# Seven block products in place of eight for 20 of the 22 gate and up column pairs of a SwiGLU, in a float32 decoder layer on one core

## The reference, cut to what matters

```python
def swiglu(x, w_gate, w_up, w_down):
    return (jax.nn.silu(x @ w_gate) * (x @ w_up)) @ w_down

for l in range(DEPTH):                                    # DEPTH is 1
    mix = hybrid_mixer(x, ...)                            # pooling, RG-LRU, short conv, gates
    x = layer_norm(ALPHA * x + mix, ln_g[l, 0], ln_b[l, 0])
    xa = memory_cross_attention(x, mem, ...)
    x = layer_norm(ALPHA * x + xa, ln_g[l, 1], ln_b[l, 1])
    ff = swiglu(x, ffn_w_gate[l], ffn_w_up[l], ffn_w_down[l])
    x = layer_norm(ALPHA * x + ff, ln_g[l, 2], ln_b[l, 2])
```

## Time and profile before

| | us |
|---|---|
| median of 3 runs | 1055.01 (1054.86 to 1055.73) |
| the profiled execution | 1056.62 |
| its span | 1054.7 |
| PE busy | 1040.6 (99%) |
| PEld busy | 878.9 (83%) |
| DVE busy | 509.9 (48%) |
| ACT busy | 388.3 (37%) |
| POOL busy | 44.7 (4%) |
| HBM read | 108.09 MB, 104 GB/s over the span |

### The profile page before, as it was taken

One profiled execution on the slowest core, in us unless ns is written; L12 is line 12 of the kernel. 1 busy time (PEld: TensorE's weight loads), 2 busy tenths in 40 slices (PEclk: granted clock), 3 DMA queues, 4 the chain that ended last, 5 costly groups with the idle time before them and its releaser, 6 DMA issues.

```text
span 1054.7 us, 12863 instructions
## 1 busy us (share of the span) xinstructions
PE 1040.6 (99%) x5020; PEld 878.9 (83%) x5020; DVE 509.9 (48%) x709; ACT 388.3 (37%) x527; POOL 44.7 (4%) x37
## 2 busy tenths in 40 slices
PE   8999999999999999999999999999999999999997
PEld 7888888888888888888889998898888888888886
DVE  4668585876432423344865564752222322243336
ACT  4455646355422222233543352542222222232222
POOL 2000000000000000000400000130000000000000
PEclk9999999999999999999999999999999999999999
DMA  5324233142432332325143331243323232222311
GB/s 203 106 82 133 80 99 119 60 122 77 160 120 80 98 101 80 120 80 212 68 160 121 120 120 41 80 159 98 102 82 117 80 115 84 98 101 81 118 41 80
DMA packets 88706, 110.65 MB, mean 105 GB/s; under 512 B 2125, under 2 KB 81121, under 8 KB 88673
## 3 DMA queue, kind: packets, MB, share of 16 engines
q1 hardware_dynamic: 86704, 103.82, 30.3%
q0 software_dynamic: 1824, 6.32, 1.7%
q10 hardware_dynamic: 144, 0.05, 0.0%
HBM read 108.09 MB, written 2.10 MB: 104 GB/s over the span
## 4 chain that ended last, share of the span: by engine, by line
PE 95%; DVE 2%; ACT 1%; POOL 1%; issue 1%; DVEq 0%; POOLq 0%
PE ps L462 32%; PE ps L464 31%; PE ps L463 31%; PE ps L491 1%; POOL wl L425 1%; DVE xnat L1142 1%; DVE xT_l L1100 0%; ACT ps L851 0%; PE ps L696 0%; DVE probs L1133 0%; ACT wh L825 0%; POOL rows L418 0%; DVE wl L1092 0%; DVE xnat L1123 0%; ACT xT_h L831 0%
## 5 line engine op out<-in xcount | busy, mean ns | idle before, releaser
L1092 DVE TENSOR_TENSOR wl<-raw,wh 128x1024 fp32r<-128x1024 f32 (+1 forms) x185 | 221.2, 1200 | 407.7 <-ACT wh L825 405.9
L825 ACT ACTIVATE wh<-raw 128x1024 fp32r<-128x1024 f32 (+1 forms) x192 | 198.8, 1041 | 493.2 <-PE ps L464 477.5
L462 PE MATMUL ps<-xT_h,wh 128*128 128x512 f32 (+1 forms) x976 | 370.9, 380 | 2.1 <-DVE xT_l L1100 1.3
L464 PE MATMUL ps<-xT_h,wl 128*128 128x512 f32 (+1 forms) x976 | 369.9, 379 | 0.0
L463 PE MATMUL ps<-xT_l,wh 128*128 128x512 f32 (+1 forms) x976 | 369.9, 379 | 0.0
L462 PEld LDWEIGHTS ps<-xT_h,wh 128*128 128x128 f32 x976 | 184.0, 189 | 36.9 <-DVE xT_l L1100 2.4
L464 PEld LDWEIGHTS ps<-xT_h,wl 128*128 128x128 f32 x976 | 184.0, 188 | 34.4
L463 PEld LDWEIGHTS ps<-xT_l,wh 128*128 128x128 f32 x976 | 184.0, 189 | 34.3
L462 PE MATMUL ps<-wh,st_h 128*128 128x512 f32 x304 | 118.8, 391 | 0.0
L463 PE MATMUL ps<-wl,st_h 128*128 128x512 f32 x304 | 118.3, 389 | 0.0
L464 PE MATMUL ps<-wh,st_l 128*128 128x512 f32 x304 | 118.3, 389 | 0.0
(11 more groups left out here) (198 smaller groups left out, 980.1 us busy)
## 6 DMA issues: line engine op xcount, KB each, us to landing
raw<-in_w_in SPq DMA_DIRECT2D x31, 1024.0 KB, 5.4
raw<-in_ffn_w_gate SPq DMA_DIRECT2D x11, 1024.0 KB, 5.1
raw<-in_ffn_w_up SPq DMA_DIRECT2D x11, 1024.0 KB, 5.2
raw<-in_ffn_w_down SPq DMA_DIRECT2D x11, 1024.0 KB, 4.8
raw<-in_lru_w_out SPq DMA_DIRECT2D x4, 1024.0 KB, 4.7
raw<-in_sconv_w_out SPq DMA_DIRECT2D x4, 1024.0 KB, 5.4
raw<-in_w_mix_out SPq DMA_DIRECT2D x4, 1024.0 KB, 4.8
raw<-in_xa_w_k SPq DMA_DIRECT2D x4, 1024.0 KB, 5.1
```

The costliest lines, as they stand in the source:

```text
L462: nc.tensor.matmul(dst, st, mv_, start=start, stop=False)
L464: return nc.tensor.matmul(dst, st_lo_part, mv_, start=False, stop=stop)
L825: nc.scalar.activation(wh[:, s % SPLIT_SLOTS, 0:size], src, ACT.Copy).then_inc(w_hi.sem, 1)
L1092: nc.vector.tensor_tensor(wl[:, slot, 0:size], src, wh[:, slot, 0:size].bitcast(F32), ALU.subtract).then_inc(w_lo.sem, 1)
```

## The change

x (as its transpose: k by tokens) and the weights (k by columns) are cut into blocks: two halves of k (512 each), two halves of the tokens (256 each), two groups of 256 columns. A **set** is 512 columns of gate or of up. Written out, its four result blocks (column group x token half) take eight block products; the Winograd form of Strassen's scheme takes seven:

- weight sums for each set, by DVE in float32: s1 = a21 + a22, s2 = s1 - a11, s3 = a11 - a21, s4 = a12 - s2 (a = column group, k half);
- x sums once, by DVE: T1, T2, T3, T4 from the four x blocks;
- products P1 = a11 x11, P2 = a12 x21, P6 = s2 T2, P5 = s1 T1, P7 = s3 T3, P4 = a22 T4, P3 = s4 x22;
- results C11 = P1 + P2, and with q = P1 + P6 and r = q + P7: C21 = r + P4 (T4's sign chosen so), C22 = r + P5, C12 = q + P5 + P3.

In each product 2 column tiles x 4 k x 3 matmuls of 128x256 go into the two halves of one bank. P6, P7 and P4 accumulate on P1's bank, P3 on P5's bank; between them ACT copies the bank out (p1, q, r, each 128 x 512), and DVE reads P2's or P5's bank and adds the copy (C11, C22, C12). Even sets are gate, odd sets up, of the same columns. For gate, ACT takes SiLU in place in `gated`; for up, DVE multiplies with it in `hidden` (C21 directly from the bank). The first pair of 256 columns is computed as before, but with 256-token x blocks in both halves already. Of 22 tiles 2 stay in that form, 20 are in ten sets.

Weight steps of a set are seven in place of eight: each product's stationary block (a block or a block sum) is split by ACT and DVE through the same ring of four slots. The loads are four blocks of 512 KB per set with semaphores of their own; a12 and a22 have two buffers each (a half of `raw`, or a half of `gb`), a11 and a21 one. So the layer norm's `gb` for G is loaded at the end of F, where it was loaded at its start. Loops over F on SP, ACT, DVE and PE become straight code.

Ahead of F, ACT also keeps a float32 copy of each transposed x tile (`keep_x`, two activations of 128x512 from PSUM per tile) from which DVE makes the x sums; PE waits for the copy of tiles 0 and 1 before it writes on their banks. G's ring is shifted by two slots (74 steps in F), and its first step takes the token tiles in the order 2, 0, 3, 1.

```diff
+            def product(n, bank, x_part, fresh):
+                weights_ready("F", 0, n)
+                ...
+                for l in range(2):
+                    for k in range(4):
+                        last = mm3(ps[:, bank, l * 256:(l + 1) * 256],
+                                   h_[:, k, l * P:(l + 1) * P], l_[:, k, l * P:(l + 1) * P],
+                                   mh[:, k, :], ml[:, k, :], fresh and l == 0 and k == 0, k == 3, shared=True)
+                last.then_inc(weights_used.sem, 1)
...
-            with pe.Fori(1, F_ITERS) as i:
-                pe.wait_ge(silu_full.sem, silu_full.done(i * 2 - 1))
-                col_unit("F", i, 0, 0, xT_h, xT_l)
-                pe.wait_ge(h_full.sem, h_full.done(i * 2 - 1))
-                col_unit("F", i, 1, 2, xT_h, xT_l)
+            pe.wait_ge(x_kept.sem, x_kept.done(2 * TT - 1))
+            product_1(0)
+            for s in range(F_SETS):
+                final = s == F_SETS - 1
+                if not final:
+                    product_2(s)
+                pe.wait_ge(chain.sem, chain.done(3 * s))
+                ...
+                product(f_step(s, "P6"), a_bank(s), T2, False)
+                ...
+                if s >= 2:
+                    pe.wait_ge(c_sum.sem, c_at(s - 2, "C12"))
+                product(f_step(s, "P5"), d_bank(s), T1, True)
+                pe.wait_ge(chain.sem, chain.done(3 * s + 1))
+                ...
+                product(f_step(s, "P7"), a_bank(s), T3, False)
+                if final:
+                    product_2(s)
+                else:
+                    product_1(s + 1)
+                pe.wait_ge(chain.sem, chain.done(3 * s + 2))
+                ...
+                product(f_step(s, "P4"), a_bank(s), T4, False)
+                pe.wait_ge(c_sum.sem, c_at(s, "C22"))
+                product(f_step(s, "P3"), d_bank(s), x_blocks[1, 1], False)
```

ACT, ahead of F and in the sets:

```diff
             deviation(1, 0, 2)
             deviation(1, 1, 4)
-            turned(20, 0, 2, xT_h, P)
+            turned_x(0, 2)
             split("E", 0, 5)
+            keep_x(0, 2)
             deviation(1, 2, 6)
-            turned(22, 1, 4, xT_h, P)
+            turned_x(1, 4)
             split("E", 0, 6)
             split("E", 0, 7)
             split("F", 0, 0)
+            keep_x(1, 4)
             deviation(1, 3, 0)
...
+            for s in range(F_SETS - 1):
+                gate, nxt = s % 2 == 0, s + 1
+                near_end = nxt == F_SETS - 1
+                next_high(nxt, "P1")
+                if not gate:
+                    gate_c(s - 1, "C12", 0, 1)
+                keep_q(s)
+                next_high(s, "P4")
+                if gate:
+                    gate_c(s, "C11", 0, 0)
+                next_high(s, "P3")
+                keep_r(s)
+                next_high(nxt, "P6" if near_end else "P2")
+                ...
+                keep_chain(nxt, "P1", p1, a_bank(nxt))
+                next_high(nxt, "P5" if near_end else "P6")
+                if gate:
+                    gate_c(s, "C22", 1, 1)
+                    ...
+                    nc.scalar.activation(gate_part(1, 0), two(ps[:, a_bank(s), :]),
+                                         ACT.Silu).then_inc(silu_full.sem, 1)
+                next_high(nxt, "P7" if near_end else "P5")
+                next_high(nxt, "P2" if near_end else "P7")
```

DVE in the sets, and its order in the last one:

```diff
+            for s in range(F_SETS - 1):
+                ...
+                c_11(s)
+                next_low(nxt, "P1")
+                sum_4(s)
+                if up:
+                    h_of(s, "C11", 0, 0)
+                next_low(s, "P4")
+                sum_1(nxt)
+                next_low(s, "P3")
+                sum_2(nxt)
+                c_22(s)
+                next_low(nxt, "P6" if near_end else "P2")
+                sum_3(nxt)
+                next_low(nxt, "P5" if near_end else "P6")
+                if up:
+                    h_of(s, "C22", 1, 1)
+                    h_21(s)
+                next_low(nxt, "P7" if near_end else "P5")
+                c_12(s)
+                next_low(nxt, "P2" if near_end else "P7")
+                if up:
+                    h_of(s, "C12", 0, 1)
+            final = F_SETS - 1
+            sum_4(final)
+            ...
+            c_22(final)
+            split("G", 0, -3)
+            h_of(final, "C22", 1, 1)
+            stage(hidden[:, 0, :], 2 * KT, 0)
+            c_11(final)
+            split("G", 0, -2)
+            h_of(final, "C11", 0, 0)
+            stage(hidden[:, 1, :], 2 * KT + 1, 1)
+            h_21(final)
+            split("G", 0, -1)
+            stage(hidden[:, 2, :], 2 * KT + 2, 2)
+            c_12(final)
+            h_of(final, "C12", 0, 1)
```

SP, for each set from the third on:

```diff
+            for s in range(2, F_SETS):
+                sp.wait_ge(s_sum.sem, s_at(s - 2, 4))
+                sp.wait_ge(w_lo.sem, w_lo.done(F0 + f_step(s - 2, "P2")))
+                block_load(a12(s), s, 0, 1, a12_in(s)[0])
+                sp.wait_ge(w_lo.sem, w_lo.done(F0 + f_step(s - 2, "P4")))
+                block_load(a22(s), s, 1, 1, a22_in(s)[0])
+                sp.wait_ge(s_sum.sem, s_at(s - 1, 3))
+                sp.wait_ge(w_lo.sem, w_lo.done(F0 + f_step(s - 1, "P1")))
+                block_load(a21(s), s, 1, 0, a21_in(s)[0])
+                block_load(a11(s), s, 0, 0, a11_in(s)[0])
```

More of the change, by code:

```diff
@@ L199, in hybrid_layer @@
         res_in = ctx.enter_context(nc.semaphore("res_in"))
+        block_in = [ctx.enter_context(nc.semaphore(f"block_in{n}")) for n in range(6)]
         gb_in = ctx.enter_context(nc.semaphore("gb_in"))
@@ new lines, in f_step, with f_used, s_at, c_at @@
+        def f_step(s, product):
+            if product == "P1":
+                return F_FIRST if s == 0 else F_FIRST + 1 + F_SET * (s - 1) + 4
+            order = "P2 P6 P5 P7 P1 P4 P3" if s < F_SETS - 1 else "P6 P5 P7 P2 P4 P3"
+            return F_FIRST + 1 + F_SET * s + order.split().index(product)
+        def f_used(s, product):
+            return weights_used.done(F0 + f_step(s, product))
+        def s_at(s, n):
+            return s_sum.done(4 * s + n - 1)
+        def c_at(s, name):
+            order = ("C11", "C22", "C12") if s < F_SETS - 1 else ("C22", "C11", "C12")
+            return c_sum.done(3 * s + order.index(name))
@@ new lines, in silu_at, with h21_at, a_bank, b_bank @@
+        def silu_at(s, name):
+            return silu_full.done(2 + 4 * (s // 2) + ("C11", "C22", "C21", "C12").index(name))
+        def h21_at(s):
+            return h_full.done(2 + 4 * (s // 2) + 2)
+        def a_bank(s):
+            return (1, 6)[s % 2]
+        def b_bank(s):
+            return (7, 2)[s % 2]
+        def d_bank(s):
+            return (0, 3)[s % 2]
+        def two(ap):
+            return ap.rearrange("p (l t) -> p l t", l=2)
+        def gate_part(row, tok):
+            return gated[:, 2 * row:2 * row + 2, tok * 256:(tok + 1) * 256]
@@ L659, in last_four @@
                         for n in range(4):
[L660 removed]
+                            last = accumulate_half(phase, s0 + n, bank, t, half, False, n == 3)
                         if half == 0:
@@ new lines, in sum_ready, with t_high, keep_chain @@
+            def sum_ready(s, n):
+                return s_sum.sem, s_at(s, n)
+            def t_high(n, dst, src):
+                act.wait_ge(t_sum.sem, t_sum.done(n))
+                nc.scalar.activation(dst[0], xf[:, src], ACT.Copy).then_inc(t_hi.sem, 1)
+            def keep_chain(s, product, dst, bank):
+                act.wait_ge(weights_used.sem, f_used(s, product))
+                nc.scalar.activation(dst[:], ps[:, bank, :], ACT.Copy).then_inc(chain.sem, 1)
+            w_high(f_step(0, "P1"), a11(0), a11_in(0))
@@ new lines, in c_12, with h_of @@
+            def c_12(s):
+                gated_free(s, "C12")
+                dve.wait_ge(weights_used.sem, f_used(s, "P3"))
+                dve.wait_ge(chain.sem, chain.done(3 * s + 1))
+                nc.vector.tensor_tensor(c_part(s, 0, 1), two(ps[:, d_bank(s), :]), two(q_sum[:]),
+                                        ALU.add).then_inc(c_sum.sem, 1)
+            def h_of(s, name, row, tok):
+                dve.wait_ge(silu_full.sem, silu_at(s - 1, name))
+                dve.wait_ge(c_sum.sem, c_at(s, name))
+                part = up_part(s, row, tok)
+                nc.vector.tensor_tensor(part, part, gate_part(row, tok), ALU.mult).then_inc(h_full.sem, 1)
```

391 lines of the change are left out of this document (322 added, 69 removed).

## The result

The changed kernel takes 1028.43 us (median of 4 runs, 1027.43 to 1028.89); the kernel before, beside it, 1054.93 (4 runs, 1054.52 to 1055.73). Ratio 0.9744, 95% interval 0.9732 to 0.9757: 26.5 us faster, where 14.9 were forecast. The direction was right.

A forecast was written before the change was run, and what follows sets the result against it. The kernel was taken as a TensorE (PE) stream, busy 99% of the span. Profiled 1056.62 - 16.0 (products) + 1.07 (front edge) = 1041.7; that execution lay 1.6 above the median, giving 1040.1 us, range 1038 to 1047.

The forecast's parts named there:

- Main term: PE stream in the F loop: 1680 half-wide matmuls at 0.1200, 201.6 us in place of 217.6, so -16.0 us.
- PE's spacing in products above 0.1200: Sign against the forecast: product matmuls spaced wider than 0.1200 us without a wait, from a shared PSUM bank or short groups.
- 5.9% dearer per column: 128x256 matmul against 128x512: 0.1200 to 0.2267 us, 0.529 and not 0.5, returning about half the saved eighth.
- The Trainium skill's figures: Issue gaps of 518 cycles for 512 columns and 262 for 256 (estimated 216 and 109 ns), implying 24 us saved.
- The prediction's other estimate from that section, 98 ns: Sustained price at 256 columns, taken halfway between 131 ns at 512 and 81 at 128; loop 39 us longer.
- DVE and ACT keep up: Added vector and scalar work in each 20.16 us set hides behind PE; copies 2.1 us early; cost 0.
- Transfers 0: Weight loads per set, four 512 KB blocks for two of 1 MB, cost 0; upper bound 0.5 a set.
- Front edge: Start of phase F: keep_x(0)'s two ACT copies delay PE's step 1 by 1.07 us; bounds 0 to 2.2.
- Preparation and back edge 0: x sums and set 0 before the products (least slack 2.5 us), and handover to the down projection (1.0 early), cost 0.
- Rivals 1, 2, 4: 1: wait each set, 4 us, chance 0.12; 2: dearer front edge, 2 to 5 us, 0.06; 4: DVE stretched, 0.02.
- Rival 4: In the sets, DVE work 22% longer makes a set exceed 21.76 us; 1057 at 25%, with waits; chance 0.02.
- Rival 3: In the straight-code products PE starves for instructions, about 13 packets, deciding from 1.2 us standstill each; 1061 at 1.6; chance 0.03.

The follow-up runs named there:

- e1: The changed kernel without the pads, so the streamed x blocks start at multiples of 256 bytes; 1040.69 us (4 runs).
- f1: The changed kernel itself run again, nothing altered; 1028.6 us (5 runs, 1027.64 to 1029.53).
- e9: The changed kernel with keep_x(0) moved ahead of the weight step before it; 1029.91 us (1026.78 to 1034.64).
- e10: The changed kernel with keep_x(0) ahead of the weight step and attention operands memT and kT at 192 bytes; 1033.08 us (1026.36 to 1036.81).
- e6: The changed kernel with the weight tiles wh and wl also moved 192 bytes, x blocks left at 192 (relative 0); 1049.04 us (1 run).
- f2: The changed kernel with keep_x(0) ahead of the weight step and set 0's q copy before the next set's first high part; 1027.73 us (5 runs).
- e3: The changed kernel with pads of 32 floats in place of 48, x at 128 bytes; 1043.16 us (1 run).

## Why the prediction was wrong

- **Main term** ("Ten sets: 1680 x 0.1200 = 201.6 us", -16.0). This step failed. The count was right, and so was the mechanism, seven products for eight in an unbroken PE stream. The price was mis-sized: it was 0.1133, and the term -27.1. The prediction took the price of a 128x256 matmul from rows in which both operands begin at a multiple of 256 bytes and gave it to matmuls whose x the change puts 192 bytes past one. Without the pads the term is -16.0 (e1). It named "PE's spacing in products above 0.1200" as what would prove it wrong, and didn't weigh that it could be below. The 1040.69 without the pads, against the 1040.1, says that the other terms were about right, and that the miss is this price.
- "5.9% dearer per column", by which about half of the saving goes back: true at 0 (288 periods for 256 columns, 32 over). At 192 it is 16 over, the same as the 544 - 512 = 32 of a full one per column, so the scheme keeps its full eighth (190.4 / 217.6 = 0.875).
- **The Trainium skill's figures** ("TensorE: Matmul & The Clock Gate", section "Back-to-back issue gap"; 262 cycles for 256 columns, an estimated 109 ns): the prediction rejected them against 0.1200. The runs show 272 to 288 cycles by place, so the page's 262 lies below all of them. (The prediction's other estimate from that section, 98 ns, is the value a third of the way from 128 to 512 columns, where 256 lies, and not halfway as it says.) The same page (section "Step-by-step: what each phase is for") says that loading weights takes no read bandwidth from a running matmul. A price that goes by where the two operands lie relative to each other speaks against two reads that never meet, but that is an argument: no run here shows the conflict itself.
- **DVE and ACT keep up**: right. DVE 163 (near 170), ACT 103 (near 105), although a set lasted 19.05 us and not 20.16. The q copy's slack of about 2 us, the tightest by hand, is where the only late start came, 0.11 us, and in the profile of f1 not even that one.
- **Transfers 0**: right but for that late block.
- **Front edge** +1.07: measured +0.94, by the same chain (ACT's copies at 683.14, high parts after them, POOL's low part, PE's step 1). e9 takes it back: the edge is 3.48 there, against 3.50 before.
- **Preparation and back edge 0**: right. The distance at both ends of the products is that of their inside.
- **Rivals 1, 2, 4** didn't occur. (Rival 4's 22% doesn't follow from the prediction's own figures: an up set, 18.3 us of DVE, fills 21.76 at 19% more.) **Rival 3** neither: 13 instruction packets came in 709.7 to 900.1 (about 13 foreseen) with PE busy 190.40 of 190.40. The queue's line (kind, packets, MB, share):
```profile
q8 instruction: 13, 0.21, 0.4%
```
- **The range** (1038 to 1047) had no lower end for the unknown price: all weight was on what could be late. The operands of a product are new tiles in new places, so their price was unseen and needed a bound below as well; a figure for it was there, half of a 512-wide one, 0.2267 / 2 = 0.1133, which makes 190.4 us. That this is just what came is seen afterwards only: at the other places the price lay between.

**Open.** Why the place matters: whether the two reads conflict, and on what. What decides which of the two prices holds at 192, and at 64. Whether products at 64 can run at 0.1133. The runs of e9 between the two groups (1029.8 and 1030.0) have a mean granted clock of 0.995, where the others have 0.999. e10's profiled run has 0.995 too, and its trace shows where from: the granted clock is 0.50 from 11.2 to 18.1 us, and the first 24 half-wide matmuls take 5.3 us there, against 2.95 in e9's profile. Taking 2.3 us off would put the two runs at 1027.5 and 1027.7, near the fast one, 1026.8. This is an estimate; they have no profile of their own.

## What to carry to other kernels

Take a matmul's price from rows with the same shape and the same placement of both operands: the start of the streamed tile less the start of the stationary one, within 256 bytes, moved the price of a 256-wide one by 6% here, and a wrong place cost a 512-wide stream 3%. Read it from distances between starts, since at the upper clock the duration column stays at 0.28 whatever the price. In a diff, an allocation that holds nothing is a change like any other; and where a kernel is 99% one engine's stream, the unit price times the count needs a range on both sides.

## What the runs showed of the hardware

- The price goes by relative place, and does not rise or fall steadily with it (table above): 272 to 288 periods for 256 columns, 544 to 560 for 512.
- Moving everything by the same 192 bytes changes nothing: 1055.01 us, 0.2267 and 0.1200.
- One place can have two lasting prices, 0.1133 and 0.1178: 192 has both in e9's products, and 64 both in e6's K projection. In e9 a delay of PE by 0.16 us (distances of 0.16 and 0.22 in place of twice 0.11, at 719.1) stood at the change from one to the other. The changed kernel's delay of 0.11 us at 720.56 left the price as it was.
- 1680 matmuls with their weight loads in straight code, one every 0.1133 us, were fed without a gap (190.40 us in f1 and f2).
- A stretch at half clock early in a run (e3: 11.4 to 18.2 us, 128x256 matmuls 0.213 apart) cost 2.5 us. It came in some profiled runs and not in others of nearly the same kernel.
